# Rotary items of the hybrid part: the permutation as two fp32r matmuls of high and low parts, and the cosine product from the bank

## What is computed

```
def partial_rope(x, cos, sin):
    xr = x[..., :ROPE_DIM].astype(jnp.float32)
    x1, x2 = xr[..., :ROPE_DIM // 2], xr[..., ROPE_DIM // 2:]
    rot = jnp.concatenate([x1 * cos - x2 * sin, x2 * cos + x1 * sin], axis=-1)
    return jnp.concatenate([rot.astype(x.dtype), x[..., ROPE_DIM:]], axis=-1)
...
    dq = partial_rope(dq.reshape(B, S, DIFF_HEADS, 2, dh).transpose(0, 2, 3, 1, 4), cos, sin)
    dk = partial_rope(dk.reshape(B, S, DIFF_HEADS, 2, dh).transpose(0, 2, 3, 1, 4), cos, sin)
...
    nq = partial_rope(nq.reshape(B, S, NSA_HEADS, dh).transpose(0, 2, 1, 3), cos, sin)
...
                          partial_rope(kv_heads(ks), cos, sin), kv_heads(vs),
                          partial_rope(kv_heads(kw), cos, sin), kv_heads(vw), gates,
```

## Time and profile before

| what | value |
|---|---|
| median of 3 runs | 2453.79 us (2452.72 to 2454.97) |
| the profiled execution | 2452.42 us |
| its span | 2450.6 us, 30755 instructions |
| PE, PEld | 2396.7 us (98%), 1942.1 us (79%) |
| DVE | 896.4 us (37%) |
| ACT | 989.0 us (40%) |
| POOL | 961.5 us (39%) |
| granted PE clock, mean | 0.994 of full speed |

### The profile page before, as it was taken

The page is one execution under the profiler, slowest core; times in us unless marked ns, Lnnn a source line. Parts: engine busy times, 40 slices in busy tenths (PEclk is TensorE's granted clock), DMA queues, the critical chain, the costliest instruction groups (busy, mean ns, idle before and its releaser), DMA issues.

```text
span 2450.6 us, 30755 instructions
## 1 busy us (share of the span) xinstructions
PE 2396.7 (98%) x11435; PEld 1942.1 (79%) x11435; DVE 896.4 (37%) x1118; ACT 989.0 (40%) x1636; POOL 961.5 (39%) x422
## 2 busy tenths in 40 slices
PE   8989999999999999999999999999999989999998
PEld 6868888888877778888878888888877658888887
DVE  6985344420322214444410422210457862322201
ACT  7764333321566634433321622321434564322212
POOL 5834444444322214444444344444232102444443
PEclk9999999999999999999999999999999999999999
DMA  5112322222211112322222222222321102222222
GB/s 184 69 45 93 112 100 97 94 95 95 78 60 55 59 61 95 112 95 101 96 95 95 87 94 94 96 92 95 152 69 64 35 1 78 103 94 95 95 94 94
DMA packets 58756, 215.32 MB, mean 88 GB/s; under 512 B 6448, under 2 KB 6448, under 8 KB 58416
## 3 DMA queue, kind: packets, MB, share of 16 engines
q1 hardware_dynamic: 55440, 199.96, 23.6%
q10 hardware_dynamic: 3232, 14.16, 1.6%
HBM read 211.99 MB, written 2.10 MB: 87 GB/s over the span
## 4 chain that ended last, share of the span: by engine, by line
PE 89%; ACT 5%; DVE 4%; issue 1%; DMA 0%; SPq 0%; DVEq 0%; ACTq 0%
PE banks L461 17%; PE banks L463 17%; PE banks L462 17%; PE banks L487 9%; PE banks L488 9%; PE banks L489 9%; PE banks L498 1%; PE banks L744 1%; PE banks L860 1%; ACT lg L1331 1%; ACT lg L1333 1%; ACT spH L1342 1%; PE banks L731 1%; PE banks L755 1%; PE banks L903 1%
## 5 line engine op out<-in xcount | busy, mean ns | idle before, releaser
L419 POOL TENSOR_TENSOR wL<-raw,wH 128x1024 fp32r<-128x1024 f32 x369 | 898.3, 2436 | 1452.0 <-ACT wH L1056 1451.9
L1056 ACT ACTIVATE wH<-raw 128x1024 fp32r<-128x1024 f32 x371 | 393.1, 1060 | 1119.2 <-PE banks L463 607.6
L461 PE MATMUL banks<-xH,wH 128*128 128x512 f32 (+1 forms) x1976 | 762.6, 386 | 13.0 <-DVE xL L1567 10.6
L463 PE MATMUL banks<-xH,wL 128*128 128x512 f32 (+1 forms) x1976 | 756.5, 383 | 0.0
L462 PE MATMUL banks<-xL,wH 128*128 128x512 f32 (+1 forms) x1976 | 756.4, 383 | 0.0
L461 PEld LDWEIGHTS banks<-xH,wH 128*128 128x128 f32 x1976 | 372.1, 188 | 91.0 <-DVE wL L1572 10.6
L463 PEld LDWEIGHTS banks<-xH,wL 128*128 128x128 f32 x1976 | 372.0, 188 | 72.8
L462 PEld LDWEIGHTS banks<-xL,wH 128*128 128x128 f32 x1976 | 372.2, 188 | 71.8 <-issue 0.7
L487 PE MATMUL banks<-wH,hH 128*128 128x512 f32 x704 | 278.1, 395 | 3.5 <-DVE tmp L1681 3.5
L489 PE MATMUL banks<-wL,hH 128*128 128x512 f32 x704 | 277.8, 395 | 0.0
L488 PE MATMUL banks<-wH,hL 128*128 128x512 f32 x704 | 277.8, 395 | 0.0
(11 more groups left out here) (248 smaller groups left out, 2397.2 us busy)
## 6 DMA issues: line engine op xcount, KB each, us to landing
raw<-ws SPq DMA_DIRECT2D x371, 512.0 KB, 3.2
w1b<-w ACTq DMA_DIRECT2D x2, 2048.0 KB, 11.4
tmp<-rows ACTq DMA_DIRECT2D x7, 512.0 KB, 4.3
b_row<-rows ACTq DMA_DIRECT2D x5, 512.0 KB, 4.6
tmp<-xT SPq DMA_DIRECT2D x8, 256.0 KB, 7.3
xr<-xN ACTq DMA_DIRECT2D x1, 2048.0 KB, 8.5
out<-xr SPq DMA_DIRECT2D x4, 512.0 KB, 2.6
pf<-pT ACTq DMA_DIRECT2D x2, 512.0 KB, 3.3
```

What stands on the lines that cost most here:

```text
L419: pool.tensor_tensor(wL[:, j, :], raw[:, j, :], fp(wH[:, j, :]), ALU.subtract).then_inc(low_ready, 1)
L461: pe.matmul(bank, wH[:, slot, cols], rh, start=start, stop=False)
L463: return pe.matmul(bank, wL[:, slot, cols], rh, start=False, stop=stop)
L1056: act.activation(wH[:, c % SLOTS, :], raw[:, c % SLOTS, :], ACT.Copy).then_inc(high_ready, 1)
```

## The change

For the rotary items, step 2 and what follows become:

- ACT rounds the bank, scaled, to fp32r: `preH` (`item_high`, new). This stands in ACT's queue ahead of `high_after` of the same item, and waits for the item's projection and, from the second rotary item on, for the permutation of the rotary item before, since there is one `preH`.
- DVE's take waits for `preH` (`pre_high`) and is two instructions from the bank: the low part, bank times scale minus `preH`, to `preL`, and the cosine product, bank times scale times cosine table, to `pre`. Both are of the form SCALAR_TENSOR_TENSOR. The first take also waits for the rotary tables.
- PE's permutation is two fp32r matmuls into one bank, `preH` and then `preL` against `permR`, a copy of the permutation in fp32r that ACT makes once at the start of the kernel.
- DVE's finish is the sine product and the sum; the cosine product from SBUF (L1883) and the semaphore `rot_ready` are gone.

`b_row` is now an overlay; `preH` lies over its first half, `preL` and `permR` are new memory.

```diff
@@ tensors
-        b_row = sb("b_row", [P, D])
+        b_row, = overlay([("b_row", [P, D], F32)])
+        pre_parts = sb("pre_parts", [P, 2, S], F32R)
+        preL = sb("preL", [P, S], F32R)
+        permR = sb("permR", [P, P], F32R)
+        preH = pre_parts[:, 0, :]
+        def head_scale(name):
+            return DH ** -0.5 if name in ("dq", "nq") else 1.0
@@ PE, second_step
                 pe.wait_ge(item_read[b], TAKEN[i])
                 if ITEMS[i][0] == "rope":
-                    mm = pe.matmul(ps[b], cc("perm"), pre[:, ROPES.index(i) % 2, :], start=True, stop=True)
+                    pe.wait_ge(pre_low, ROPES.index(i) + 1)
+                    pe.matmul(ps[b], permR[:], preH, start=True, stop=False)
+                    mm = pe.matmul(ps[b], permR[:], preL[:], start=False, stop=True)
@@ ACT
+            act.activation(permR[:], cc("perm"), ACT.Copy).then_inc(const_ready, 1)
...
+            def item_high(i):
+                kind, name, h = ITEMS[i]
+                if kind != "rope":
+                    return
+                r = ROPES.index(i)
+                act.wait_ge(chunk_done, c0 + i + 1)
+                if r:
+                    act.wait_ge(second_done, second_count(ROPES[r - 1]))
+                act.activation(preH, ps[item_bank(i)], ACT.Copy, scale=head_scale(name)).then_inc(pre_high, 1)
...
             for i in range(5):
+                item_high(i)
                 high_after(c0 + i)
             copy_turned_item(3)
             for i in range(5, 7):
+                item_high(i)
                 high_after(c0 + i)
...
+            item_high(8)
             high_after(c0 + 8)
...
                 a = 10 + 3 * h
+                item_high(a)
                 high_after(c0 + a)
                 if ITEMS[a - 1][0] == "turn":
                     copy_turned_item(a - 1)
                 exps(h)
+                item_high(a + 1)
                 high_after(c0 + a + 1)
                 if h:
                     copy_output(h - 1)
                     head_inverse_std(h - 1)
+                item_high(a + 2)
                 high_after(c0 + a + 2)
                 copy_turned(h)
+            item_high(NITEMS - 1)
             high_after(c0 + NITEMS - 1)
@@ DVE, take_item
                     r = ROPES.index(i)
-                    if r >= 2:
+                    if r == 0:
+                        dve.wait_ge(rope_loaded, 16)
+                    elif r >= 2:
                         dve.wait_ge(roped, r - 1)
-                    dve.tensor_scalar(pre[:, r % 2, :], ps[b], DH ** -0.5 if name in ("dq", "nq") else 1.0, None,
-                                      ALU.mult).then_inc(item_read[b], 1)
+                    dve.wait_ge(pre_high, r + 1)
+                    dve.scalar_tensor_tensor(preL[:], ps[b], head_scale(name), fp(preH), ALU.mult, ALU.subtract)\
+                        .then_inc(pre_low, 1)
+                    dve.scalar_tensor_tensor(pre[:, r % 2, :], ps[b], head_scale(name), ropeT[:, 0, :], ALU.mult, ALU.mult)\
+                        .then_inc(item_read[b], 1)
@@ DVE, finish_rope
-                if r == 0:
-                    dve.wait_ge(rope_loaded, 16)
-                else:
+                if r:
                     dve.wait_ge(roped, r)
                 dve.wait_ge(second_done, second_count(i))
                 dve.tensor_tensor(rot, ps[b], ropeT[:, 1, :], ALU.mult).then_inc(item_read[b], 1)
-                dve.tensor_tensor(pre[:, r % 2, :], pre[:, r % 2, :], ropeT[:, 0, :], ALU.mult).then_inc(rot_ready, 1)
-                dve.wait_ge(rot_ready, r + 1)
                 dve.wait_ge(item_read[b], FINISHED[i])
                 dve.tensor_tensor(dst, pre[:, r % 2, :], rot, ALU.add).then_inc(roped, 1)
```

More of the change, by code:

```diff
@@ L297, in build_block @@
         roped = sem("roped")
-        rot_ready = sem("rot_ready")
+        pre_high = sem("pre_high")
+        pre_low = sem("pre_low")
         blocks_ready = sem("blocks_ready")
```

## The result

The changed kernel takes 2460.28 us (median of 12 runs, 2456.15 to 2463.85), the kernel before 2453.76 us (12 runs, 2450.39 to 2456.58). The ratio is 1.0028, 95% interval 1.0019 to 1.0036: slower by 0.28%, just outside the predicted range and above the bound of 0.2%. The profiled execution of the changed kernel took 2457.8 us, 5.4 us more than that of before.

The account below looks back on a forecast made before the run. PE was taken to bound the kernel (89% of the chain); 5.6 us saved less 7.6 us taken back by waits gave net +2.0, 2454.4 us profiled, 2455.8 us as median, range 2451 to 2460 us.

Parts of the forecast that it names:

- What a permutation costs PE: Rotary items on PE: two fp32r matmuls, 0.46 us, replace a float32 one of 0.86; 0.40 us an item, 5.6 us saved.
- D: Rival: permR does not change the arithmetic rate, 0.43 us a matmul, 2461.4 us; C and D beyond +4.9 us together 18%.
- What DVE gains: DVE's rotary work: 23 us of records go, mostly waiting; the final add stays and inherits the wait for POOL's splits.
- B: Rival: items 2 to 5 cost nothing, DVE gets in between splits; 2453.8 us; 17% with what lies between it and A.
- Place 1, item 4: Items 2 to 5: low part of item 4 ends near 1789.1, PE waits 0.85 us more, delay +2.05 us.
- rival C: PE's clock falls in new gaps, ahead of items 12 and 22; 1.7 us once, 2457.5 us; beyond +4.9 with D 18%.
- Place 2: Heads 0 to 3: the third projection waits for the sine product; delay +1.45 us at item 13, +2.43 at item 22.
- S: Start of the permutation of a head's first rotary item; the third projection was predicted at S + 3.25 us, before S + 3.09.
- Place 3: The end, from item 22's take to the pairs' first maximum: DVE is the chain, 0.5 us shorter, delay +1.9 us.
- A: Rival: all of the gain arrives, DVE and ACT keep up everywhere; 2448.2 us, chance 10%.

Follow-up runs that it names:

- experiment 1: Changed kernel with ACT's bank copy of item 2 ahead of the rounding of chunk +4, which waits for its DMA; ratio 1.0013 to the kernel before.
- 4: Changed kernel with filler matmuls on PE, 5 ahead of the turn of item 3 and 10 ahead of item 4's permutation; ratio 1.0026 to the kernel before.
- 5: The kernel of 4 with 14 more filler matmuls on PE ahead of the projection of item 12 in head 0; ratio 1.0011 to the kernel before.
- 3: Changed kernel with item 2's bank copy early on ACT and the sine products ahead of the next takes on DVE; 2448.64 us, ratio 0.9979.
- 9: The kernel of 3 with DVE's take of item 4 ahead of finish_copy(1); 2445.19 us, ratio 0.9971 to the kernel before.
- 10: The kernel of 3 run again unchanged, as reference on the same chip; 2445.69 us, ratio 0.9979 to the kernel before.
- experiment 2: Changed kernel with DVE's sine product ahead of the next take, in the heads and for the last two items; ratio 1.0004 to the kernel before.

## Why the prediction was wrong

What bounds the kernel, which queues would make PE wait, and that the 5.6 us of saved matmuls would be more than given back: right. The sum said 7.6 us given back, the trace has 12.0 (5.6 + 6.38). By its steps:

**What a permutation costs PE**: right. Step 0.23 us, so D is out.

**What DVE gains**: right that the sum inherits the wait (2.90 us where it had 2.77), and that the block adds stand in splits: 3.62 us for the first two, 1.74 for the last two. The take of item 3 ended at 1782.04 us on the clock of before (1781.22 + 0.82), predicted 1782.05, and PE waited 1.01 us there, predicted 1.05. So B is wrong: POOL got in between two block adds that wait for nothing. Its second split was already issued while the first add ran. The two adds of the 3.62 us one by one, and the split:

```profile
1773.82 1.03 DVE L1903 TENSOR_TENSOR tmp<-kcvc,par 64x248 f32<-64x248 f32 x1
1774.78 2.66 DVE L1903 TENSOR_TENSOR tmp<-kcvc,par 64x248 f32<-64x248 f32 x1
```

```profile
1774.43 2.64 POOL L428 TENSOR_TENSOR wL<-raw,wH 128x1024 fp32r<-128x1024 f32 x1
```

The Trainium skill (SBUF — State Buffer, Who interferes with whom) says that the order of issue decides which of the two engines blocks. The trace agrees: the split's row starts at 1774.43 us, the second add's at 1774.78. The condition that the prediction gave for B, that DVE's next add starts before POOL's next split, was not met.

**Place 1, item 4, is the step that failed**, and with it the choice to leave the clock (rival C) out of the sum: 1.4 and 1.7 us of the 4.4 us that were not predicted. It had PE's wait at 0.85 us; it was 1.86, and the permutation began at 1790.44 us on the clock of before where the prediction has 1789.15: 1.3 us late. Two things were missed. First, 0.7 us on DVE. I let it "go on with add (0.6)": that is the sum's price beside an idle POOL, but the next split began at 1781.93 and the sum at 1781.98, so it took 2.90. The eight adds of finish_copy(1) behind it then had no split to stand through and took 3.5 us instead of the 4.6 that I gave them, so sum and adds took 6.3 us (1781.98 to 1788.28), not 5.2. (The terms in the text give 1788.6 for the low part's end, not the "near 1789.1" that stands there; that slip hid 0.5 us of the 1.1 and leaves the 0.7 to the trace's 1789.8.) Second, 0.6 us on PE. I had PE released by the low part, but it waits for `item_read` too, which is now on the second instruction of the take: the wait's row names L1887, and the permutation began behind its end (1789.57) and not behind the low part's (1788.97).

**Rival C was right in kind, and I had its place and its count wrong.** I looked for it ahead of items 12 and 22, where the gaps are longest, and let it decide only from a second stretch. It came once, behind the 1.86 us wait of item 4, at the 1.7 us that the rival had for one stretch. In experiment 1, where the waits at items 3 and 4 are all but gone, and in 4, where they are filled, it stands behind the 2.8 us wait of head 0; it is gone where both places are filled (5) or mended (3). My case against it (the work ahead of the gaps is dense) is refuted. The Trainium skill (TensorE: Matmul & The Clock Gate, HAM oscillation — how this bites in real kernels) warns of TensorE's idle gaps above a certain length; the longest here, 2.8 us, is below it, so that by this rule there would have been no fall. The measurement decides.

Ahead of head 0's maximum the account closes. All delays here are from timeline to timeline, with 0.82 us between the two clocks. The permutation of item 4 began at 1786.98 us before and 1789.62 after: 3.46 us late, predicted 2.05, so 1.4 us. (The 1787.14 of the prediction is the chain's time for the same instruction, 0.16 us later than the timeline's.) The turn of item 5 (1793.32 and 1797.26) is 4.76 us late: the 0.40 of the permutation saved, 1.7 lost to the clock. Items 6 and 8 give back their 0.8 us, and the scores of head 0 begin 3.95 us late (1826.99 and 1830.12). The last 0.2 us of the 4.17 are DVE's: before, it waited 1.02 us for the scores ahead of the first maximum; now its take, two instructions behind ACT's copy, runs until 1831.70 and the maximum stands behind it.

**Place 2**: head 0 was right: from its maximum to that of head 1 the delay grew by 0.65 us, predicted 0.60. Heads 1 and 2 had the wrong sign: +0.08 us a head in place of -0.24, twice 0.3 us. The sine product releases PE at S + 3.39 (1864.07 to 1867.46), not at S + 3.25: from PE's last step to ACT it is 0.26 us, predicted 0.20, and from ACT to DVE 0.13, for which I had estimated 0.05. And before it was not S + 3.09, a sum of two lengths from the chain, but S + 3.01 by the timeline that I used for S elsewhere. So the third projection starts 0.38 us later than before and not 0.16: 0.2 of the 0.3 us. The rest is in steps of under 0.05 us. A step whose sign turns on 0.16 us should have had its hand-offs as bounds.

**Place 3**: its rows came in the order forecast, with the sum of item 21 standing 1.89 us in the split, but the delay at the pairs' maximum exceeds that of head 3 by 1.40 us where 1.03 was predicted. PE's timelines separate the steps. Its delay grows by 0.39 us ahead of item 21 (1913.82 before, 1918.14 after), predicted 0.16, and by 1.53 us ahead of item 22 (1921.23 and 1927.11), predicted 1.30: the hand-off of place 2 twice more. The end gives back 0.28 us in place of 0.43, and the 0.2 us by which DVE's take held back the maximum of head 3 are gone here.

**A** is wrong in this order. It is a fair account of what the change can do in another: experiments 3, 9 and 10 have 5.0 to 5.6 us less in the stretch.

Left open: the two ratios of the changed kernel, 1.0028 and 1.0045, in two sets of runs with intervals that overlap and stretches 0.07 us apart; and why the clock in the pairs was lower in experiment 2. A second `preH`, which would free ACT's copy from the permutation before, wasn't tried.

## What to carry to other kernels

When an instruction of one more engine is put into a hand-off, find out first what stands ahead of it in that engine's queue, since its wait becomes the hand-off's: here the copy took 0.6 us and stood behind a wait of 9 us for a DMA. Put what frees a resource ahead of what takes the next one, and try such an order again after each change: the same swap cost 2.6 us in the old kernel and gave 6.6 us in the new one. And where work is moved, move the competitor's as well: a cost read beside an idle engine (0.6 us) is not the cost beside a busy one (2.9 us).

## What the runs showed of the hardware that I had not expected

- TensorE's clock fell to 1.2 GHz for 3.4 us behind a wait of 1.86 us in work that was dense otherwise (one of 1.01 us ended 6.5 us before it began), and did not fall behind one of 2.8 us in the same execution. With the first filled, it fell behind the second.
- DVE's instructions with two SBUF inputs let POOL in between even where nothing but their order separates them: two block adds, 1.07 us together with POOL idle, took 3.62 us, since a split was issued at 1774.43 us, ahead of the second add at 1774.78.
- Hand-offs in head 1 of the changed kernel: PE's last step to ACT's start 0.26 us (1864.53 to 1864.79), ACT's end to DVE 0.13 us (1865.39 to 1865.52), DVE's end to PE 0.05 us (1867.41 to 1867.46).
